# A hybrid decoder step: gate couples of one kind, 1024-byte loads, another order on VectorE in the conv turns, and adaLN pairs moved within a turn

## The reference, cut to what matters

```
mod  = silu(c) @ w_ada + b_ada                      # adaLN: shift, scale, gate, twice
h    = rmsnorm(x) * (1 + sc1) + sh1
bg, cg, ua, q, k, v, r, lr, ga, gb = split(h @ w_in)    # w_in is 1024 x 8208
conv = causal_dwconv3(cg * ua);  y_a = bg * conv
o    = GLA recurrence over q, k, v with decay from lr (4 heads, chunks)
y_b  = rmsnorm(o) * silu(r)
x    = x + g1 * rmsnorm((sigmoid(ga) * y_a + sigmoid(gb) * y_b) @ w_out)
h2   = rmsnorm(x) * (1 + sc2) + sh2
a, g = split(h2 @ w_up);  x = x + g2 * rmsnorm((gelu(dwconv3(a)) * g) @ w_down)
```

## Time and profile before

| what | value |
|---|---|
| median of 3 runs | 1019.81 us (1019.51 to 1022.11) |
| profiled execution, its own time | 1020.2 us |
| its span in the trace | 1018.5 us |
| mean granted TensorE clock | 0.978 |
| TensorE busy (matmul) | 963.3 us, 95% |
| VectorE busy | 629.5 us, 62% |
| ScalarE busy | 458.7 us, 45% |
| GpSimd busy | 169.3 us, 17% |

### The profile page before, as it was taken

The page is one execution under the profiler, slowest core; times in us unless marked ns, Lnnn a source line. Parts: engine busy times, 40 slices in busy tenths (PEclk is TensorE's granted clock), DMA queues, the critical chain, the costliest instruction groups (busy, mean ns, idle before and its releaser), DMA issues.

```text
span 1018.5 us, 18472 instructions
## 1 busy us (share of the span) xinstructions
PE 963.3 (95%) x7479; PEld 873.1 (86%) x7479; DVE 629.5 (62%) x928; ACT 458.7 (45%) x767; POOL 169.3 (17%) x101
## 2 busy tenths in 40 slices
PE   6999799899877888999999999999999999999997
PEld 4889799788766777889999889999999999888886
DVE  3687677300565677543654768998999998760204
ACT  4466345534232232444355343755665566533212
POOL 2010000353222222322335200000000000003330
PEclk9999999999998898999999999999999999999999
DMA  9686854743944465754743604133333322322222
GB/s 332 222 101 83 64 103 64 186 127 63 151 134 129 124 165 149 126 94 108 156 120 109 196 1 124 42 104 94 94 86 102 104 84 84 124 68 84 82 66 93
DMA packets 145029, 115.58 MB, mean 113 GB/s; under 512 B 11225, under 2 KB 121585, under 8 KB 144945
## 3 DMA queue, kind: packets, MB, share of 16 engines
q1 hardware_dynamic: 144849, 114.38, 46.4%
q10 hardware_dynamic: 96, 0.04, 0.0%
HBM read 107.02 MB, written 7.35 MB: 112 GB/s over the span
## 4 chain that ended last, share of the span: by engine, by line
PE 82%; DVE 6%; issue 5%; SPq 2%; DMA 2%; ACT 2%; POOL 1%; DVEq 0%; POOLq 0%; ACTq 0%
PE pair L2480 26%; PE pair L2387 22%; PE pair L2553 16%; PE pair L2822 5%; PE pair L2377 2%; SPq L811 2%; PE pair L2608 1%; DVE cv L1825 1%; DMA raw_c<-in_w_in 1%; DVE suf L620 1%; PE pair L2317 1%; PE pair L2635 1%; DMA x_tok<-in_x_prompt 1%; DVE ext L1819 1%; PE pair L2545 1%
## 5 line engine op out<-in xcount | busy, mean ns | idle before, releaser
L965 POOL TENSOR_TENSOR w_lo<-raw,w_hi 128x1024 fp32r<-128x1024 f32 x41 | 102.1, 2492 | 641.4 <-ACT w_hi L1040 641.4
L2387 PE MATMUL pair<-h_hi,w_hi 128*128 128x288 f32 x624 | 149.8, 314 | 0.5 <-POOL w_lo L969 0.4
L2387 PE MATMUL pair<-h_lo,w_hi 128*128 128x288 f32 x624 | 142.0, 302 | 0.0
L2387 PE MATMUL pair<-h_hi,w_lo 128*128 128x288 f32 x624 | 141.5, 301 | 0.0
L2387 PEld LDWEIGHTS pair<-h_hi,w_hi 128*128 128x128 f32 x624 | 105.8, 196 | 18.2 <-issue 16.0
L2387 PEld LDWEIGHTS pair<-h_lo,w_hi 128*128 128x128 f32 x624 | 105.8, 195 | 0.0
L2387 PEld LDWEIGHTS pair<-h_hi,w_lo 128*128 128x128 f32 x624 | 105.2, 194 | 0.0
L1040 ACT ACTIVATE w_hi<-raw 128x1024 fp32r<-128x1024 f32 x54 | 56.9, 1057 | 104.6 <-PE pair L2547 80.2
L2480 PE MATMUL pair<-h_hi,w_hi 128*128 128x288 f32 x348 | 103.3, 297 | 0.0
L2480 PE MATMUL pair<-h_hi,w_lo 128*128 128x288 f32 x348 | 102.7, 295 | 0.0
L2480 PE MATMUL pair<-h_lo,w_hi 128*128 128x288 f32 x348 | 102.7, 295 | 0.0
(11 more groups left out here) (397 smaller groups left out, 2133.0 us busy)
## 6 DMA issues: line engine op xcount, KB each, us to landing
raw_c<-in_w_ada SPq DMA_DIRECT2D x32, 512.0 KB, 4.8
raw<-in_w_in SPq DMA_DIRECT2D x208, 64.0 KB, 3.1
raw_c<-in_w_in SPq DMA_DIRECT2D x208, 64.0 KB, 3.4
raw<-in_w_up SPq DMA_DIRECT2D x24, 512.0 KB, 3.9
raw<-in_w_down SPq DMA_DIRECT2D x22, 512.0 KB, 3.7
raw_up<-in_w_up SPq DMA_DIRECT2D x20, 512.0 KB, 3.8
ada_first<-in_w_ada SPq DMA_DIRECT2D x16, 512.0 KB, 9.8
raw<-in_w_in SPq DMA_DIRECT2D x8, 512.0 KB, 4.8
```

The lines of the kernel that those rows point to most:

```text
L965: pool.tensor_tensor(lo, raw_tile(n)[:, :], hi.bitcast(F32), ALU.subtract).then_inc(S("w_lo_done"), 1)
L2387: ins = pe.matmul(bank[pair][:, half, 0:HALF], w[:, i, :], x[:, i, HALF * half:HALF * half + HALF], start=i == 0 and p == 0, stop=i == KT ...
```

## The change

It does five things. Gate couples are now of one kind: couple c holds two neighbouring tiles of ga (c even) or of bg (c odd), so that both lie in 256 adjacent columns, and a load is 8 DMAs of 128 KB in runs of 1024 bytes, released together by the fourth low part of couple c-2. The sigmoids run in the ga turn and the gate products in the bg turn behind it. On ScalarE the stacked samples come ahead of the copy of V+2. On VectorE `take_mod(j-1)` moves to between the queries and the keys of the next level, the first score group of the next level is taken behind the taps and ahead of the prefix sum, and in turn 0 the last group is taken right behind the conv input. On TensorE both adaLN pairs of a turn stand behind its last half tile and `mod_back`. The diff, cut to its core (waits whose counts follow from it are left out where they repeat):

```diff
@@ load_early @@
-            def load_early(c, x):
+            def load_early(c):
                 if c < 2:
-                    cols = IN_Q + DK * (2 * c + x)
+                    cols = IN_Q + 2 * DK * c
                     sp.wait_ge(S("w_lo_done"), 2 * c + 2)
                 else:
-                    cols = (IN_GA, IN_BG)[x] + P * (c - 2)
-                    sp.wait_ge(S("w_lo_done"), early_fill(c - 2, 2 + x) + 1)
-                dst, src = kc(early_raw(c, x)), in_cols(cols)
+                    cols = (IN_GA, IN_BG)[c % 2] + 2 * P * (c // 2 - 1)
+                    sp.wait_ge(S("w_lo_done"), early_fill(c - 2, 3) + 1)
+                dst, name = (raw23, "raw_c_in2") if c % 2 else (raw01, "raw_in0")
                 for i in range(KT):
-                    sp.dma_start(dst[:, i, :], src[:, i, :]).then_inc(S(early_landed[c, x][0]), 16)
+                    sp.dma_start(dst[:, i, :], w_in[P * i:P * i + P, cols:cols + 2 * P]).then_inc(S(name), 16)
...
@@ scalar @@
-            def gate_sigmoid(c):
+            def gate_sigmoids(c):
+                second = sga[1][:, HALF:T]
                 act.wait_ge(S("c_sum"), 3 * c + 3)
-                act.activation(sga[:, :], sga[:, :], ACT.Sigmoid).then_inc(S("sga_done"), 1)
+                act.activation(sga[0][:, :], sga[0][:, :], ACT.Sigmoid).then_inc(S("sga_done"), 1)
+                act.activation(second, second, ACT.Sigmoid).then_inc(S("sga_done"), 1)
+
+            def last_sigmoid(c):
+                act.wait_ge(S("ring_free"), early_product(c, 6))
+                act.activation(sga[1][:, 0:HALF], one_bank(2 + c % 2)[:, 0:HALF], ACT.Sigmoid).then_inc(S("sga_done"), 1)
...
-                if c >= 2:
-                    gate_sigmoid(c)
+                if c >= 2 and c % 2 == 0:
+                    gate_sigmoids(c)
...
+                    elif c % 2 == 0:
+                        last_sigmoid(c)
...
-                else:
-                    high(TILE_V + 2)
...
             act.activation(h_smp_hl[:, :, 64:P], h_lo[:, :, SEQ:T].bitcast(F32), ACT.Copy).then_inc(S("stacked"), 1)
+            high(TILE_V + 2)
...
@@ vector @@
             def early_gate(c):
-                j = c - 2
-                dve.wait_ge(S("sga_done"), j + 1)
-                dve.wait_ge(S("c_sum"), 3 * c + 2)
-                dve.tensor_tensor(y_a[:, j, HALF:T], ec22[:, :], sga[:, HALF:T], ALU.mult).then_inc(S("ya_done"), 1)
+                first, second = early_out(c, 0), early_out(c, 1)
+                dve.wait_ge(S("sga_done"), 3 * (c // 2))
+                dve.wait_ge(S("c_sum"), 3 * c + 3)
+                dve.tensor_tensor(first, first, sga[0][:, :], ALU.mult).then_inc(S("ya_done"), 1)
+                dve.tensor_tensor(second[:, HALF:T], second[:, HALF:T], sga[1][:, HALF:T], ALU.mult).then_inc(S("ya_done"), 1)
                 dve.wait_ge(S("ring_free"), early_product(c, 6))
-                dve.tensor_tensor(y_a[:, j, 0:HALF], one_bank(2 + c % 2)[:, 0:HALF], sga[:, 0:HALF], ALU.mult) \
+                dve.tensor_tensor(second[:, 0:HALF], one_bank(2 + c % 2)[:, 0:HALF], sga[1][:, 0:HALF], ALU.mult) \
                    .then_inc(S("ya_done"), 1)
...
-                if c >= 2:
+                if c >= 2 and c % 2:
                     early_gate(c)
...
             for j in range(KT):
                 for e in (0, 2, 4):
-                    for i in after_tile(j, e):
-                        take_item(dve, i)
+                    if e > 0 or j == 0:
+                        for i in after_tile(j, e):
+                            take_item(dve, i)
                 if j + 1 < KT:
-                    level_products(dve, j + 1)
+                    level_queries(dve, j + 1)
+                if j > 0:
+                    take_mod(dve, j - 1)
+                if j + 1 < KT:
+                    level_keys(dve, j + 1)
                 else:
                     dve.wait_ge(S("exps"), 1)
                     dve.tensor_tensor(k[:, :, :], k[:, :, :], suf[:, :, :], ALU.mult).then_inc(S("decayed"), 1)
                 conv_input(j)
-                for i in after_tile(j, 6):
-                    take_item(dve, i)
+                for e in (6, 7):
+                    for i in after_tile(j, e):
+                        take_item(dve, i)
                 if j + 1 < KT:
                     level_suffix(dve, j + 1)
                 mix_taps(j)
                 if j + 1 < KT:
+                    for i in after_tile(j + 1, 0):
+                        take_item(dve, i)
                     level_prefix(dve, j + 1)
-                if j > 0:
-                    take_mod(dve, j - 1)
                 conv_gate(j)
-                for i in after_tile(j, 7):
-                    take_item(dve, i)
@@ tensor @@
-                    elif e % 4 == 3:
-                        ada_pair(2 * j + e // 4)
+                    elif e == 7:
+                        ada_pair(2 * j)
+                        ada_pair(2 * j + 1)
```

More of the change, by code:

```diff
@@ L197, in layer_program @@
     ep5 = place("ep5", [P, HALF], offset=g_at + 66688)
-    ec22 = place("ec22", [P, HALF], offset=g_at + 67840)
-    sga = place("sga", [P, T], offset=g_at + 92672)
+    sga = [place(f"sga{i}", [P, T], offset=g_at + 92672 + 2304 * i) for i in range(2)]
     qd = place("qd", [P, HEADS * T // 2], offset=g_at + 46080)
@@ L395, in layer_program @@
     for c in range(EARLY):
[L396 to L399, removed]
+        name = "raw_c_in2" if c % 2 else "raw_in0"
+        so_far[name] += 16 * KT
+        early_landed[c] = name, so_far[name]
     landed_at += [None] * (4 * EARLY)
@@ L416, in raw_landed, with early_raw, early_source @@
         return landed_at[n if n < TILE_DN else n - TILE_DN + TILE_UP + 4]
-    def early_raw(c, x):
-        return raw_c[2 + x] if c % 2 else raw[x]
+    def early_raw(c, x, blocks=slice(0, KT)):
+        return (raw23 if c % 2 else raw01)[:, blocks, P * x:P * x + P]
+    def early_source(c, slot):
+        if slot == 1:
+            return kc(es12)
+        return early_raw(c, 1, upper) if slot == 3 else early_raw(c, 0)
+    lower, upper = slice(0, 4), slice(4, KT)
     def early_fill(c, slot):
@@ L612, in level_products, with level_keys @@
         dve.tensor_tensor(dst, dst, src, ALU.mult).then_inc(S("qd_done"), 1)
+    def level_keys(dve, lv):
+        B = LEVELS[lv]
         if B > 1:
@@ L1118, in early_high @@
                 if slot in (0, 3):
-                    name, count = early_landed[c, slot // 3]
+                    name, count = early_landed[c]
                     act.wait_ge(S(name), count)
@@ L1123, in early_high @@
                 act.wait_ge(S("ring_free"), early_fill(c, slot) - 3)
-                src = (early_raw(c, 0)[:, :], es12[:, :], early_raw(c, 0)[:, :], early_raw(c, 1)[:, 512:1024])[slot]
-                dst = w_hi[slot][:, 0:512] if slot == 3 else w_hi[slot][:, :]
-                act.activation(dst, src, ACT.Copy).then_inc(S("w_hi_done"), 1)
+                blocks = lower if slot == 3 else slice(0, KT)
+                act.activation(kc(w_hi[slot])[:, blocks, :], early_source(c, slot), ACT.Copy).then_inc(S("w_hi_done"), 1)
             def early_u1(c):
@@ L1695, in early_sums12 @@
             def early_sums12(c):
-                for x in range(2):
-                    name, count = early_landed[c, x]
-                    dve.wait_ge(S(name), count)
+                name, count = early_landed[c]
+                dve.wait_ge(S(name), count)
                 if c > 0:
                     dve.wait_ge(S("w_lo_done"), early_fill(c - 1, 1) + 1)
-                a11, (a21, a22) = early_raw(c, 0)[:, 0:512], (early_raw(c, 1)[:, 0:512], early_raw(c, 1)[:, 512:1024])
-                dve.tensor_tensor(es12[:, 0:512], a21, a22, ALU.add).then_inc(S("s_add"), 1)
+                a11, a21, a22 = early_raw(c, 0, lower), early_raw(c, 1, lower), early_raw(c, 1, upper)
@@ L1715, in early_low, with early_out @@
-                cols = slice(0, 512) if slot == 3 else slice(0, 1024)
+                blocks = lower if slot == 3 else slice(0, KT)
                 dve.wait_ge(S("w_hi_done"), early_fill(c, slot) + 1)
-                dve.tensor_tensor(w_lo[slot][:, cols], src, w_hi[slot][:, cols].bitcast(F32), ALU.subtract) \
+                dve.tensor_tensor(kc(w_lo[slot])[:, blocks, :], early_source(c, slot),
+                                  kc(w_hi[slot])[:, blocks, :].bitcast(F32), ALU.subtract) \
                    .then_inc(S("w_lo_done"), 1)
+            def early_out(c, x):
+                if c < 2:
+                    return q[:, 2 * c + x, :]
+                return y_a[:, 2 * (c // 2 - 1) + x, :] if c % 2 else sga[x]
@@ L1720, in early_c11 @@
             def early_c11(c):
-                dst = q[:, 2 * c, 0:HALF] if c < 2 else sga[:, 0:HALF]
+                dst = early_out(c, 0)[:, 0:HALF]
                 dve.wait_ge(S("a_done"), 3 * c + 1)
                 dve.wait_ge(S("ring_free"), early_product(c, 1))
-                if c > 2:
-                    dve.wait_ge(S("ya_done"), 2 * (c - 2))
```

(6 more changed lines are left out.)

27 lines of the change are left out of this document (15 added, 12 removed).

## The result

The changed kernel takes **974.79 us** (median of 4 runs, 974.25 to 975.65) against 1020.14 (1019.51 to 1022.11, 4 runs) of the kernel before on the same chip: ratio 0.9553, 95% interval 0.9537 to 0.9570. The forecast was 974.0, range 964 to 990. The profiled execution took 974.86 us, its span is 973.1, and the mean granted clock rose from 0.978 to 0.997.

The account below looks back on a forecast made before the run. TensorE, busy 95% of the span, was taken as the bound, so only its holes and low-clock stretches could be won: 7.7 + 5.5 + 32.9 = 46.1 us off 1019.8 gives 973.7, forecast 974, range 964 to 990.

Parts of the forecast that it names:

- Part 1: Early stage: same-kind couples loaded in 1024-byte runs remove the stall and low clock of one slow turn, 7.7 us.
- What a 1024-byte run costs is the open quantity: Early couple loads: cost per couple between 3 and 19.4 us, 9.7 if it goes by runs; the quick side was taken.
- the row 33:36: Profile window at the end of the key loads, 1024-byte runs mixed with 2048-byte ones, 367 GB/s; evidence for quick couple loads.
- Rival B: Early stage: slow stretches stay slow in 1024-byte runs, 7.7 us lost again plus 2 for later start; 983, chance 0.11.
- Part 2: Start of the V stage: stacked samples made ahead of V+2's copy remove TensorE's wait, 5.5 us, bounds 4 and 5.6.
- Part 3: Conv turns: VectorE's new order and moved adaLN pairs shorten the stage from 181.1 to 148.2 us, 32.9 won.
- The slip that was feared: Conv turns 1 to 3: VectorE's gate slips into a GpSimd subtraction, one block of 2.3 us; 2.0 put into the sum.
- ScalarE's in-order copies hold up its exponentials: Conv turns 1 and 2: slow C1 loads make adaLN tiles late and so delay ScalarE; about 3.5 us, bounds 0 and 8.
- A: Rival, conv turns: VectorE becomes the bound and TensorE has holes again, 14 us more; 988, chance 0.17.
- C: Rival, conv turns: TensorE's take_mod wait becomes an equal wait for the keys, only 13.2 us won overall; 1007, chance 0.03.
- D: Rival, conv turns: the burst of C1 and adaLN loads takes 24.8 us a turn, 31 lost; 1038, chance 0.03.
- nothing else stands in that queue: SP's queue, conv turns: four 512 KB loads and two C1 tiles issue in one burst, wanted 15 us later.

Follow-up runs that it names:

- e1: Kernel before with same-kind couples in 1024-byte runs alone, old conv order, pair places and V+2 copy order: 1014.66 us, ratio 0.9945.
- e8: Changed kernel with each couple load split into its two column blocks, 512-byte runs, 16 DMAs in place of 8: 977.56 us, ratio 0.9575.
- e9: Kernel before, early couples of the fourth and eighth column block loading the third and seventh of GA and BG again: 1013.56 us, ratio 0.9927.
- e10: Changed kernel with C1 tiles of the fourth and eighth column block loaded from the third and seventh: 970.22 us, ratio 0.9503.
- e2: As e1, with the copy of tile V+2 behind the stacked samples; conv turns as in the kernel before: 1006.47 us, ratio 0.9863.
- e11: Changed kernel with six memsets on VectorE between take_mod and the key product in turns 1 to 6: 996.76 us, ratio 0.9751.
- e4: Changed kernel with the adaLN pairs at their old places (mid-turn and behind the last half tile), VectorE's new order kept: 997.25 us, ratio 0.9776.
- e6: Changed kernel with a turn's two C1 loads ahead of its four adaLN loads in SP's queue: 971.11 us, ratio 0.9506.
- e5: Changed kernel with the first adaLN pair of a turn behind the third half tile, the second behind the last: 985.66 us, ratio 0.9670.

## Why the prediction was right, and where it was not

The sum was 46.1 us; the medians differ by 45.3. By the starts of the stages, 8.5 us were won ahead of V, 4.4 in V (57.0 to 52.6) and 32.5 in the conv turns, where 7.7, 5.5 and 32.9 were forecast.

**Part 1: right size, wrong cause.** The early stage won 8.5 us at the start of V, where 7.7 were claimed; alone it leaves 6.7 (e1), since the hole at V grew. The step "What a 1024-byte run costs is the open quantity" asked the wrong question: the length of the run changes neither the rate nor the turns of this stage (e8), and the row 33:36 was of other columns. Slow is the fourth column block of a kind. Before, a couple was the fourth block of GA and the fourth of BG, 1.05 MB at 54 GB/s. Now a couple is the third and the fourth of one kind, and a slow half beside a quick one moves at 102; two turns share what one had to bear. e9 shows it in the kernel before, without the change. Rival B (the slow stretches stay slow) was half true: they do, the couples are merely mixed otherwise. That the 7.7 came out was luck of this mixing.

The Trainium skill, DMA: Bandwidth & Descriptors, section Latency and other measured facts, ties slow copies to the row pitch, and says that a pad of 192 bytes doesn't help. The pitches that it gives start at 512 KiB (207 GB/s) and are slow from 2 MiB on (164); the pitch of 32,832 bytes isn't among them, and the prediction stretched the rule to it. The trace agrees only as far as this, that such a matrix has slow loads, and that the change didn't mend them. And at one and the same pitch e9 and e10 lose the slow stretches by moving 128 columns, so the pitch alone doesn't decide.

**Part 2: right mechanism, other size.** 5.5 were claimed; against the kernel before the V stage is 4.4 shorter, and the edit itself is worth 6.9 (spans) to 8.2 (medians) behind part 1 (e1 to e2), because part 1 brings TensorE to V 8.5 sooner and V+2's load only 6.6 (ScalarE's copies at 185.36 and 191.96). The working had taken the hole of the kernel before, 4.15; behind part 1 it was 6.0. The two parts together were 14.9 by medians, against 13.2.

**Part 3: right stage, one step missed.** 148.2 us worked out, 148.6 measured. The turn without holes (16.9) held: 16.7 to 16.8 in turns 4 and 6. So did the keys' 2.5 us to spare (2.3 to 2.6 in e11). The slip that was feared didn't come: no GpSimd block reached the path, and its 2.0 were counted for nothing. The slow loads were 5.1 us in turn 1 and 1.0 in turn 5, not 3.5, and came otherwise than "ScalarE's in-order copies hold up its exponentials": TensorE's own hole of 3.49 and the low clock behind it. These two errors cancel but for 0.6. The last `mod_back` is 8.07 us after its last half tile (7.9 claimed), though only 2.5 of it were idle, since C2's first half tile runs within.

What the working never said is why the pairs moved. It gave this move no term of its own and listed no waiter for the row copy; yet e4 shows that without this move 22.5 of the 31.7 us are not there. The total was right only because the turn was summed from TensorE's own work, which includes both moves, and VectorE's round was held against `mod_back` at the turn's end, as the new place of the pair has it. A prediction for the order alone would have been 20 us too low, as the expectation of e4 was.

**The rivals.** A (VectorE the bound) didn't come, but e11 shows how near it is: with 4.2 us more it costs 22, and its trace has a gate product of 2.90 us (329.05) that takes 0.68 in the changed kernel, beside a GpSimd subtraction (328.17, 3.22 us). C (`take_mod` wait turns into another of VectorE) is what happens with the order alone, with the row copy in place of the keys (e4). D (the burst) was right in kind for turns 1 and 5 and small in size. The step "nothing else stands in that queue", of SP's queue, was wrong: the C1 tiles of turn 3, the slow ones, stood behind adaLN loads that waited for the pairs, with the DMA engines idle for 16 us. That cost 3.7 (e6).

Open: what it is about the address of a column block that makes it slow. Other traffic isn't needed: in e6 the same tiles move 54 GB/s at a share of 1.01 (232 to 236 us) with no other load beside them. The eighth block was moved along with the fourth, not alone. That TensorE's holes end with the landing of an instruction packet is in the rows; that this packet had been asked for earlier and stood behind the loads is argued from its lateness, since no row shows when it was asked for, nor for which engine it is.

## What to carry to other kernels

List every wait that hangs on the end of a chain that you shorten, not only the one that stands first: here two moves that win 9 and 3 us alone win 32 together, since each hides behind the other's wait. When a load is slow, change what it reads before its form: the length of the runs and the number of DMAs were innocent, the column block was not. And put the loads that need nothing ahead of those that wait in one queue.

## What the runs showed of the hardware

- Loads of one matrix at one pitch run at 54 GB/s at a full DMA share for one block of 128 columns (kernel before, 104 to 120 us), and at 90 GB/s at less than half of the share (0.46) right behind it; 512 or 1024 bytes a run made no difference (102 GB/s both).
- TensorE can stop in the middle of a row of matmuls with no semaphore: at one place of its program for 3.49 us in the changed kernel, 4.01 in e5, 3.92 in e11, 0.75 in e6 and not at all in e10. Such a hole ends 1.2 to 1.5 us after a 16 KB packet of the instruction queue q8 has landed, and it was long where slow loads filled the DMA engines.
- A short hole can cost about as much again through the clock: the 24 matmuls behind holes of 1.9 us (e6, e11) and of 4.3 (e11) took 4.84 to 4.95 us in place of 3.38, at a mean granted clock of 0.64 to 0.67; behind one of 1.6 (e11) they took 3.38, at 1.00.
